# First stage, its hand-over to the projections, and seven hand-written orders changed in a two-block transformer kernel

## What is computed

```python
def ada_params(cvec, w, b):
    m = jax.nn.silu(cvec) @ w + b
    return jnp.split(m, 3, axis=-1)          # shift, scale, gate

def modulate(x, g, shift, scale):
    return rms_norm(x, g) * (1.0 + scale) + shift

# layer 0: x (1024 rows) and ctx (256 rows) both modulated, then projected
lam = exp(sum(q1 * k1)) - exp(sum(q2 * k2)) + lam_init
proj = h @ w_in                              # f, q, k, v and a gate
kc, vc = split_kv(hc @ w_in[:, K0:G0], k_norm)
...
# layer 1: u = cg * xt; conv over 3 rows; (bg * conv * silu(g)) @ w_out
# second block, feed-forward: causal conv of x @ w_in, (silu(gate) * val) @ w_out
```

## Time and profile before

| | us |
|---|---|
| median of 3 runs (lowest, highest) | 1856.58 (1854.06, 1858.5) |
| the profiled execution's own time | 1857.68 |
| its span, first to last instruction | 1855.9 |
| PE busy in the span | 1774.3 (96%) |
| DVE, ACT, POOL busy | 1167.8, 800.6, 757.2 |
| first block of work, "ada" | 0 to about 50.7 |
| first projection matmul | 56.57 |

### The profile page before, as it was taken

The page is one execution under the profiler, slowest core; times in us unless marked ns, Lnnn a source line. Parts: engine busy times, 40 slices in busy tenths (PEclk is TensorE's granted clock), DMA queues, the critical chain, the costliest instruction groups (busy, mean ns, idle before and its releaser), DMA issues.

```text
span 1855.9 us, 22927 instructions
## 1 busy us (share of the span) xinstructions
PE 1774.3 (96%) x8745; PEld 1474.4 (79%) x8745; DVE 1167.8 (63%) x1315; ACT 800.6 (43%) x1244; POOL 757.2 (41%) x452
## 2 busy tenths in 40 slices
PE   5899999899999799999999999999999999999999
PEld 3688888668888688878888888987888888878887
DVE  3703876338888832965454653497666666779876
ACT  5324221346666632643333442655444444444443
POOL 0325322000000123356666531257999999920000
PEclk9899999899999999999999999999999999999999
DMA  8414113460000180212221341312232223187333
GB/s 324 149 48 117 46 46 102 177 245 1 0 0 0 46 268 32 65 57 79 69 80 57 118 155 46 94 43 73 76 91 80 91 80 91 57 310 262 138 120 124
DMA packets 162089, 188.31 MB, mean 101 GB/s; under 512 B 9231, under 2 KB 117320, under 8 KB 160840
## 3 DMA queue, kind: packets, MB, share of 16 engines
q1 hardware_dynamic: 161991, 187.00, 30.6%
HBM read 152.37 MB, written 34.60 MB: 101 GB/s over the span
## 4 chain that ended last, share of the span: by engine, by line
PE 50%; DVE 5%; ACT 2%; issue 2%; DMA 1%; POOL 0%; SPq 0%; ACTq 0%; DVEq 0%; POOLq 0%
PE ps L3039 18%; PE ps L2043 14%; PE ps L3090 10%; PE ps L2103 5%; PE ps L3390 1%; PE ps L3052 1%; DMA y_a<-y_scratch 1%; DVE cv_lo_p L130 1%; DVE up_lo_p L130 1%; DVE residual L2906 0%; DVE residual L1965 0%; ACT residual L3226 0%; DMA res_scratch<-x_nat 0%; PE ps L3056 0%; DVE residual L2945 0%
## 5 line engine op out<-in xcount | busy, mean ns | idle before, releaser
L3039 PE MATMUL ps<-up_hi_p,st_hi_p 128*128 128x512 f32 x560 | 218.0, 389 | 3.6 <-issue 2.0
L3039 PE MATMUL ps<-up_lo_p,st_hi_p 128*128 128x512 f32 x560 | 217.9, 389 | 0.0
L3039 PE MATMUL ps<-up_hi_p,st_lo_p 128*128 128x512 f32 x560 | 217.8, 389 | 0.0
L3090 PE MATMUL ps<-down_ring 128*128 128x512 f32 x924 | 210.7, 389 | 2.1 <-DVE down_ring L130 1.9
L3090 PEld LDWEIGHTS ps<-down_ring 128*128 128x128 f32 x924 | 173.2, 188 | 39.4 <-DVE down_ring L130 2.7
L130 POOL TENSOR_TENSOR in_lo<-in_raw,in_hi 128x512 fp32r<-128x512 f32 (+1 forms) x56 | 92.4, 1659 | 233.0 <-ACT in_hi L127 182.6
L2043 PE MATMUL ps<-cv_hi_p,cv_st_hi_p 128*128 128x512 f32 x392 | 153.4, 391 | 4.5 <-issue 4.5
L2043 PE MATMUL ps<-cv_lo_p,cv_st_hi_p 128*128 128x512 f32 x392 | 153.0, 390 | 0.0
L2043 PE MATMUL ps<-cv_hi_p,cv_st_lo_p 128*128 128x512 f32 x392 | 153.0, 390 | 0.0
L130 POOL TENSOR_TENSOR st_lo_p<-up_raw,st_hi_p 128x512 fp32r<-128x512 f32 x68 | 100.9, 1487 | 67.2 <-ACT st_hi_p L127 67.2
L3039 PEld LDWEIGHTS ps<-up_hi_p,st_hi_p 128*128 128x128 f32 x560 | 105.1, 188 | 26.2 <-issue 2.4
(11 more groups left out here) (377 smaller groups left out, 4209.0 us busy)
## 6 DMA issues: line engine op xcount, KB each, us to landing
up_raw<-in_ffn_w_in SPq DMA_DIRECT2D x44, 512.0 KB, 5.2
w_raw<-in_ffn_w_out SPq DMA_DIRECT2D x66, 256.0 KB, 3.0
ada_raw_rest<-in_ada_w SPq DMA_DIRECT2D x32, 512.0 KB, 6.1
cv_raw<-in_odd_w_in SPq DMA_DIRECT2D x32, 512.0 KB, 5.4
in_raw<-in_even_w_in SPq DMA_DIRECT2D x48, 256.0 KB, 2.8
y_scratch<-residual SPq DMA_DIRECT2D x22, 512.0 KB, 2.6
ada_raw<-in_ada_w SPq DMA_DIRECT2D x8, 1024.0 KB, 17.3
residual<-in_x SPq DMA_DIRECT2D x2, 2048.0 KB, 10.3
```

The source lines that it names most:

```text
L3039: last = pe.matmul(ps[:, bank(j, p), :], w[p][:, kk * P:(kk + 1) * P], x[p][:, kk, :], start=(first and w is st_hi and x is up_hi), stop=( ...
L3090: last = pe.matmul(ps[:, 4 * (i % 2) + m, :], slot[:, s, m * P:(m + 1) * P], slot[:, x, :], start=(k == 0 and s == 0 and x == 2 and DOWN[i ...
```

## The change

Line numbers below are those of the kernel before. It does this:

1. The norm statistics of x and ctx are taken from the untransposed rows by ACT (`Square` with `accum_out`, one instruction for each of 8 + 2 row tiles) and end in the same `compact` tile. The 7 DVE adds, the DVE reduction of the squared ctx, and both `tensor_mean` steps on PE go. The copies of x out of PSUM move from ACT to DVE.
2. SP's queue: only the first 7 of the 13 row loads stand ahead, ctx stands between modulation blocks 3 and 4, and the other 6 row loads and the four weight slices stand between blocks 5 and 6. The lambda loads and their arithmetic move into the second block; the exponential then stands on ACT ahead of the first qk root.
3. All four slices are split in the first block, high parts on ACT and low parts on POOL. Before, only the first high part was.
4. Tile k = 0 of x is modulated in two halves of 512 columns, and PE starts on the left half's four row tiles when that half is done.
5. Seven order edits later on: in the convolution layer `p1_copy(2)` goes behind the plain copies, the last weight splits of unit 2 and `middle_tap(0)`, and DVE's `differences(3)` goes ahead of `gated_input(0)`; in the feed-forward layer `ga_tap2(0)` goes ahead of `p1_copy(2)`; at the start of the down projection the last unit's `ga_tap2` and taps go ahead of the step parts that had stood in front of them.

```diff
                     def _(sp):
...
-                        for t, r, src in row_sources:
+                        for t, r, src in row_sources[:FIRST_ROWS]:
                             sp.dma_start(rows[r:r + src.shape[0], t, :], src).then_inc(sem("rows_in"), 16)
-                        for n, name in enumerate(("even_lambda_q1", "even_lambda_k1", "even_lambda_q2", "even_lambda_k2")):
-                            sp.dma_start(lam_in[:, n, :], a[name].broadcast_to([P, DH])).then_inc(sem("lam_in"), 16)
-                        sp.dma_start(nat[:, RT:KEYT, :], ctx_rows).then_inc(sem("ctx_in"), 16)
                         for k in range(KT):
+                            if k == 4:
+                                sp.dma_start(nat[:, RT:KEYT, :], ctx_rows).then_inc(sem("ctx_in"), 16)
+                            if k == 6:
+                                for t, r, src in row_sources[FIRST_ROWS:]:
+                                    sp.dma_start(rows[r:r + src.shape[0], t, :], src).then_inc(sem("rows_late"), 16)
+                                for n in range(RING):
+                                    load_slice(sp, n)
                             sp.dma_start(ada_raw[:, k, :], a["ada_w"][0, k * P:(k + 1) * P, 0:len(ADA_FIRST) * BANK])\
                               .then_inc(sem(f"ada_in{k}"), 16)
-                        for n in range(RING):
-                            load_slice(sp, n)
...
                         pe.wait_ge(sem("cond_ready"), 1)
+                        ada(0, 2)
+                        spread(spread_x, range(RT), "in_x_inverse").then_inc(sem("in_x_spread"), 1)
+                        ada(2, 4)
                         pe.wait_ge(sem("ctx_in"), 16)
+                        pe.wait_ge(sem("xt_copied"), KT)
...
-                        ada(3, 6)
-                        pe.wait_ge(sem("cols_copied"), 3)
-                        stats.tensor_mean(pe, KT - 1)
-                        ada(6, 7)
...
+                        ada(4, 5)
+                        spread(spread_c, range(RT, KEYT), "c_inverse").then_inc(sem("c_spread"), 1)
+                        ada(5, 6)
+                        pe.wait_ge(sem("rows_late"), 16 * (len(row_sources) - FIRST_ROWS))
+                        turn_columns(1, 3)
+                        ada(6, KT).then_inc(sem("ada_summed"), 1)
...
+                            act.activation(square[:, r % 2, :], nat[:, r, :], ACT.Square, accum_out=compact[:, r:r + 1])\
+                               .then_inc(sem(done), 1)
...
-                        high_slice(act, 0)
+                        for n in range(RING):
+                            high_slice(act, n)
+
+                    @block.gpsimd
+                    def _(pool):
+                        for n in range(RING):
+                            pool.wait_ge(sem("in_high"), n + 1)
+                            split_low(pool, in_lo[:, n, :], in_raw[:, n, :], in_hi[:, n, :], sem("in_low"))
...
+                        for k in range(KT):
+                            dve.wait_ge(sem("xt_turned"), k + 1)
+                            dve.tensor_copy(x_t[:, k, :], pair[k % 2]).then_inc(sem("xt_copied"), 1)
+                        inverted(compact[:, 0:RT], "in_x_rooted", "in_x_inverse")
...
+            def vector_first_halves(self, dve):
+                self.scale(dve, 0, LEFT, "scaled_left")
+                self.scale(dve, 0, RIGHT, "scaled")
+                dve.wait_ge(self.s("high_left"), 1)
+                self.lower(dve, 0, LEFT, "low_left")
+                dve.wait_ge(self.s("high"), 1)
+                self.lower(dve, 0, RIGHT, "low")
...
                             if n < N_SLICES and SLICES[n] == ("f", KT - 1, "f"):
+                                act.wait_ge(sem("lam_dots"), 2)
+                                act.activation(lam_exp[:, :], lam_dot[:, :], ACT.Exp).then_inc(sem("lam_exped"), 1)
                                 root(0, KEYT)
...
@@ the convolution layer, ACT and DVE @@
-                p1_copy(2)
                 for kind, side in PLAIN_OUT:
                     plain_out(1, kind, side)
                 for p in ("p3", "p4"):
                     high_stationary(act, p, 2)
-                moving_stands(act, "p4", HALF - 1)
                 middle_tap(0)
                 for g in range(2, G - 1):
-                    if g > 2:
-                        p1_copy(g)
+                    p1_copy(g)
...
                 differences(2)
+                differences(3)
                 gated_input(0)
-                differences(3)
...
@@ the feed-forward layer, ACT and DVE @@
+                ga_tap2(0)
                 p1_copy(2)
-                ga_tap2(0)
...
                 va_tap2(N - 1)
+                ga_tap2(N - 1)
                 high_pair(act, SLOTS)
-                high_pair(act, SLOTS + 1)
-                ga_tap2(N - 1)
                 silu(N - 1)
...
+                ga_taps(N - 1)
                 low_t(dve, SLOTS)
-                low_s(dve, LOW_FIRST)
-                low_t(dve, LOW_FIRST)
-                ga_taps(N - 1)
                 product(N - 1)
```

240 lines of the change are left out of this document (112 added, 128 removed).

## The result

The changed kernel takes 1845.76 us, median of 6 runs (1841.13 to 1848.77), beside 1855.62 for the kernel before in the same session (6 runs, 1854.04 to 1858.5). The ratio is 0.9942, with a 95% interval of 0.9929 to 0.9955: 9.9 us less, and 8 to 13 by the interval. The profiled execution has a span of 1845.2 us. 1848.0 was predicted.

A forecast was written before the change was run, and what follows sets the result against it. The prediction took PE's chain of waits as the bound, with the DMA engines full in the opening. Its terms, -4.0 - 3.6 - 3.1 + 0.5 + 1.2 = -9.0 us, gave 1848, range 1843 to 1854.

The forecast's parts named there:

- Opening: First block, up to the second block's start: the DMA stream ends earlier, -4.0 us, bounds -0.5 and -6.
- Hand-over: Second block's start to PE's first projection matmul: 2.3 us instead of 5.85, term -3.6 us, bounds -2.5 and -4.
- Lambda arithmetic: Exponential on ACT ahead of the qk roots: 2.8 us, covered by DVE's idle 11.13 us, so 0 us.
- Convolution: Convolution layer's opening: p4 starts 1.6 us earlier, 1.5 us of clock loss goes; -3.1 us, bounds 0 and -3.2.
- the prediction's own list of signs: Profile readings to check; wrong if block starts after 49, convolution p4 waits over 3 us, or clock behind new gaps reads 0.50.
- rival C: New waits of 2.7 and 3.0 us lower PE's clock too, first block's tail costs another 1: about 1852, chance 0.12.
- Feed-forward: Feed-forward layer's opening: new wait of 3.0 us at p2, the 2.05 at p4 goes; +0.5 us, bounds 0 and +2.
- Down projection: Start of the down projection: PE waits about 2 us at step 4; +1.2 us, bounds 0 and +3.2.
- the two ring waits: PE's waits for the down ring, 0.92 and 1.0 us, to be covered in part by the delay at step 4.
- Rival B: Opening stays bound as before, late rows cost their full 2.5 us, gain 0.5 instead of 4.0: about 1852, chance 0.13.
- rival D: New order waits add to the old ones, 10.7 us in all with the clock's loss: 1859.7, chance 0.10.
- rival E: Clock stays high over the hand-over as PE idles less, 4 us more gained: about 1844, chance 0.10.

The follow-up runs named there:

- orders_alone: The kernel before with only the seven order edits, first stage untouched: 1856.11 us, ratio to the kernel before 0.9999.
- rows_all_ahead: The changed kernel with all 13 small row loads ahead of the modulation blocks again: 1847.42 us.
- lambda_ahead: The changed kernel with the four broadcast lambda loads back between the first row loads and the modulation blocks: 1848.71 us.
- lambda_late_alone: The kernel before with only the lambda loads and their arithmetic moved to the second block: 1855.24 us, ratio to the kernel before 0.9994.
- tile0_whole: The changed kernel with tile k = 0 modulated whole, not in two halves: 1848.71 us.

## Why the prediction was right, point by point

- **Opening, -4.0 (bounds -0.5 and -6): it was -6.2 between the two profiles and -5.3 like with like** (49.82 in `orders_alone`; 0.9 is the fall of the clock in the profile of the kernel before). The block starts at 44.52, forecast 46.7. The last product stood at 40.97 (forecast 41.7), because the stream has no low stretch at all. Behind it the block's end took 3.6 us and not 4.2, and the 0.8 us for a lower clock didn't fall due: the clock was 1.00 to 46 us. Against 50.72 the term was undersized by 2.2, of which 0.7, 0.6 and 0.8 are these three, and lies just outside its own bound; like with like it was undersized by 1.3 and lies inside. Two steps of it were wrong in kind. I put the 42 GB/s down to the rows and sized the restart by their number: `rows_all_ahead` shows nothing for the rows beyond the spread, `lambda_ahead` 5.4 for the broadcasts. And I took the DMA stream for what bounded the old opening: in `lambda_late_alone` the stream ends some 3 us earlier and the block's start stays, since the statistics end just as late. That the sum came near the mark rests on the new stream's end alone, which was worked out from bytes, and on the statistics being off the path in the changed kernel; for a change to the loads alone the same reading would have promised a gain that didn't come.
- **Hand-over, -3.6: it was -3.4** (2.44 us after the start; 2.3 forecast). The sentence drawn from the Trainium skill's page "SBUF — State Buffer", "Who interferes with whom", gave POOL's absence 2 to 3 us; `tile0_whole` measures 1.9, and the halves carry 1.5.
- **Lambda arithmetic, 0**: in `lambda_late_alone`, where only this was added, the kernel's time is that of before, and from the gate products to the convolution layer it takes 484.8 us, beside 484.9 in `orders_alone`. The loads' worth lay in the opening, which I had not priced apart.
- **Convolution, -3.1: the segments give -2.9.** PE waited 2.67 us at p2 (2.7 forecast) and not at all at p4, and `middle_tap(0)` came 1.6 us earlier, as forecast. The 1.5 us that the clock should have given came in three of ten profiles (314.4 against 315.5 to 316.1). In the changed kernel's it read 0.52 behind p2, which by the prediction's own list of signs counts against it: there rival C was right at both new waits.
- **Feed-forward, +0.5: the segments give +1.4**, inside its bounds of 0 and +2. The wait of 3.0 at p2 came as forecast, and the one of 2.05 at p4 went. But the reason for the cost was another: the wait of 1.53 us at `p1_copy(3)` went too, so PE waits 0.6 us less here than before. The cost is the clock's, 0.70 in the window of the 5.7 us behind the wait, or 1.7 us, which I had only as the upper bound.

```profile
1251.00:1256.70 5.70, 5.67 (x18) 4.55 (x19) 4.61 (x4) 5.37 (x7) 4.03 (x2) 0.70 0.00 0
```

- **Down projection, +1.2: the segments give 0.** The wait of 2 us at step 4 came (2.06), and it took the place of the two ring waits, wholly and not in part.
- The sum was -9.0; the segments give -5.3 - 3.4 - 2.9 + 1.4 = -10.2, and the kernel's time -9.9. Part of the closeness is luck: the opening gave 1.3 us more than forecast and the down projection cost 1.2 less, while the hand-over and the convolution gave 0.2 less each and the feed-forward layer cost 0.9 more, so that 2.5 us of misses one way stand against 1.3 the other way. Rival B (late rows, 1852) and rival D (added waits, 1860) didn't come. Rival C came in places (the convolution's and feed-forward's new waits), and rival E didn't: the clock was 0.59 behind the hand-over until PE was kept busy.

## What to carry to other kernels

Two limits side by side hide each other: an edit that is worth nothing alone can be worth five us once the other limit is gone, so take away both before you judge either. Moving work across a barrier can be a shift and not a gain, as the four slices' loads and splits were here; look for where the same us comes back. When the parts are smaller than the spread of executions, compare segments of the profile over all kernels that share the code, and look at the clock of each before you call a difference the change's.

## What the runs showed of the hardware

- With four broadcast loads of 64 floats to 128 partitions, 32 KB each, ahead of large loads, the DMA stream ran at 28, 54 and 115 GB/s in the three microseconds from 14 us (`lambda_ahead`), and its engines were busy 22% of that time; six loads of 193 rows of 512 bytes in the same place cost nothing beyond the spread (`rows_all_ahead`: 364 GB/s from 14 to 18 us). SP needed 1.07 and 1.20 us to issue the last two in the kernel before, but went on to ctx at 10.52 and to the first modulation block at 11.05, ahead of the low stretch, so the issuing doesn't explain it.
- The lower clock comes and goes between executions of like code: in the openings of the convolution and the feed-forward layer it came behind waits of PE of about 2.0 us in 2 of 7 profiles, of 2.5 to 2.7 in 7 of 10, and of 2.9 to 4.5 us each time (11 of 11).
- Ten matmuls put into a wait of 3.46 us kept the clock at 1.00 in two kernels, and in a third with the same ten, in the same place, they ran at the lower clock themselves.
- Two DVE scales of 128x1024 took 2.48 us with GpSimd idle and 3.49 with its splits beside them; GpSimd's four splits took 4.96 and 9.01.
